# A top-4-of-32 expert layer: gathering tokens in 1 KB pieces and turning them with VectorE instead of TensorE

## Chip, cores and metric

One Trainium2 chip, one of its cores. The metric is the device time of one execution in microseconds; the median of several runs counts.

## What is computed

One layer of a hybrid encoder on 512 tokens plus 16 meta tokens, 1024 channels. A first half (one input projection, a depthwise convolution branch, an mLSTM branch, an output projection) is not touched by the change. The second half is a mixture of experts:

```python
u2 = rms_norm(h, norm_ffn_g)                          # 512 rows of 1024 count
logits = u2 @ router_w + router_b
top_val, top_idx = lax.top_k(logits, 4); gates = softmax(top_val)
# for every expert e, on the tokens that chose it:
hcat = xb @ w1[e] + b1[e]                             # 1024 -> 2048
h_glu, h_lin = split(hcat); h_glu = min(h_glu, 7); h_lin = clip(h_lin, -7, 7)
act = h_glu * sigmoid(1.702 * h_glu) * (h_lin + 1)
y = act @ w2[e] + b2[e]                               # 1024 -> 1024
out = rms_norm(h + sum over the 4 of gate * y)
```

512 tokens choose 4 of 32 experts each, so an expert gets 64 tokens on average. All weights are float32: an expert's w1 and w2 are 12 MB.

## The kernel before, in words

The program is written engine by engine, with semaphores by hand; each engine runs its own list in order. Up to about 520 us it does the first half. Then it makes `u2` (L1995, VectorE), writes it to DRAM as `u2_rows` (L522), computes logits, picks four experts for every token and gives each token a place in its expert's list (`choose`, `find_slots`).

An expert is computed on 96 slots (`SLOTS`), in three groups of 32 (`TG`). The expert loop runs once over the 32 experts. For expert n:

- TensorE, L1619: `hidden(k, t)`, 8 k-steps by 3 slot groups by 4 column groups of w1 (four products side by side in the array, 32 output partitions each), stationary `xT`, moving w1 from the ring. The first five k-steps go k by k, the last three slot group by slot group. After the fifth k-step stand the bias products (L1639, L1645), which wait for all of the last expert's `y_out` (`y_made`).
- VectorE and ScalarE turn each slot group of hidden units into `actT` (L2118 to L2131; the last step is a 32x32 block transpose, L2131).
- TensorE, L1668: `second(t)`, 32 products a slot group, moving w2. Between `second(0)` and `second(1)` stands `x_transposes(n + 1)` (L1606): eight TensorE transposes of the gathered rows `xs` [96 partitions, 1024] of the next expert. ScalarE copies them to `xT` (L1123).
- VectorE adds the bias and writes `y_out` (L2144), after POOL's step counter `idx_step` says that the last expert's scatters have landed.
- GpSimd (POOL): for each expert it copies the index columns (L754, L706), waits until `xs` has been used, gathers the rows of expert n+2 with one indirect DMA of 96 rows of 4 KB (L700), then issues three indirect DMAs that scatter `y_out` as 1 KB pieces to DRAM (L766), waits for their landing (`y_stored`, then `carrier`, L695), and goes on.
- SyncE (SP) loads the weights through a ring of 12 chunks of 1 MB, 8 of w1 (L484) and 4 of w2 (L488), each as soon as `ring_used` says that the last expert's chunk has been used.

Expert 0 has no gather: its `xT` comes from products of `u2` with a one-hot matrix of slots, `in_slot` (L1551), copied by ScalarE (L1088). Expert 1's rows are gathered with `token_now` made by VectorE (L2071). From expert 2 on, the indices come from a table in DRAM. GpSimd fills it with 16 indirect DMAs (L717), reads it back with 1 + 12 DMAs (L734, L738), and makes `token_of` and `row_of` with four arithmetic instructions (L741 to L746); only then it enters its expert loop (L754 on), whose first gather is that of expert 2.

## Time and profile before

| | us |
|---|---|
| median of 3 runs | 1619.48 (1618.56 to 1621.51) |
| profiled execution, first to last instruction (span) | 1597.8 |
| median less span (start and end around it) | 21.7 |
| TensorE busy | 1571.5 (98% of the span) |
| VectorE, GpSimd, ScalarE busy | 649.7, 444.7, 384.0 |
| data moved by DMA | 493.10 MB |

The profile shows one execution; its whole device time is not listed apart from its span, so what lies around the span is taken as the difference to the median. TensorE is busy from start to end, at full clock almost throughout. The expert loop takes from 542 to about 1575 us. A busy TensorE does not say that it works at its best, and the DMA engines are close to fully busy in the loop as well, at some 400 to 420 GB/s.

### The profile page before, as it was taken

The page shows a single profiled execution, that of the slowest core. Times are in us where ns is not written, and L with a number is a line of the kernel's source. Part 1 is how long each engine was busy: PE and PEld are TensorE (multiplying, and loading weights), DVE is VectorE, ACT ScalarE, POOL GpSimd, SP SyncE. Part 2 cuts the span into 40 slices and gives each one's busy share as a digit, 9 for nine tenths or more (in the row PEclk, how much of TensorE's full clock was granted, in tenths as well). Part 3 has the DMA queues.
Part 4 walks back from the last instruction along what each step waited for, and adds up shares of the span by engine and source line. Part 5 has one row for each costly group of instructions (what it writes and reads, how often), then busy time and mean ns, then how long its engine had stood idle before and what let it go on. Part 6 is the DMA issues. An engine that isn't in the chain of part 4 may idle for free.

```text
span 1597.8 us, 38945 instructions
## 1 busy us (share of the span) xinstructions
PE 1571.5 (98%) x16458; PEld 902.0 (56%) x16458; DVE 649.7 (41%) x1249; ACT 384.0 (24%) x601; POOL 444.7 (28%) x513
## 2 busy tenths in 40 slices
PE   7999999999999999999999999999999999999997
PEld 6998988877889644334433344334433443344334
DVE  4799898016242742224222332233222322232248
ACT  5333134346222311111111121122112111211112
POOL 7334333462433642111211111111211121112114
PEclk9999999999999999999999999999999999999999
DMA  7553242321275699999999999999999999999995
GB/s 217 159 179 112 79 144 95 90 72 51 79 294 224 204 340 406 407 416 414 412 398 410 412 409 398 414 407 408 394 411 407 410 392 404 411 412 400 403 413 236
DMA packets 129781, 493.10 MB, mean 309 GB/s; under 512 B 14379, under 2 KB 72099, under 8 KB 79973
## 3 DMA queue, kind: packets, MB, share of 16 engines
q1 hardware_dynamic: 110932, 464.61, 74.6%
q0 software_dynamic: 9168, 16.78, 3.2%
q10 hardware_dynamic: 9632, 11.03, 2.2%
q8 instruction: 35, 0.57, 0.1%
q14 instruction: 14, 0.11, 0.0%
HBM read 476.32 MB, written 24.87 MB: 314 GB/s over the span
## 4 chain that ended last, share of the span: by engine, by line
PE 95%; POOL 1%; ACT 1%; SPq 1%; DMA 1%; DVE 1%; issue 0%; POOLq 0%; DVEq 0%; ACTq 0%
PE banks L1619 41%; PE banks L1147 27%; PE banks L1668 21%; PE banks L1606 2%; DMA stage<-in_w_in_dram 1%; PE banks L1551 0%; PE banks L1639 0%; SPq L461 0%; PE banks L1506 0%; POOL h_res L787 0%; PE banks L1379 0%; POOL w_lo L624 0%; POOL w_lo L633 0%; POOL small L611 0%; SPq L447 0%
## 5 line engine op out<-in xcount | busy, mean ns | idle before, releaser
L1619 PE MATMUL banks<-w_ring,xT 128*32 128x512 f32 x6144 | 670.9, 592 | 0.1
L1619 PEld LDWEIGHTS banks<-w_ring,xT 128*32 128x32 f32 x6144 | 197.8, 110 | 431.3 <-issue 422.4
L1668 PE MATMUL banks<-w_ring,actT 128*32 128x256 f32 x6144 | 343.9, 380 | 0.0
L1668 PEld LDWEIGHTS banks<-w_ring,actT 128*32 128x32 f32 x6144 | 195.3, 110 | 144.8 <-issue 19.3
L2118 DVE TENSOR_TENSOR hid<-banks,bias 128x512 f32<-128x512 f32 x96 | 63.8, 665 | 475.6 <-PE banks L1619 475.6
L633 POOL TENSOR_TENSOR w_lo<-stage,w_hi 128x2048 fp32r<-128x2048 f32 x38 | 175.3, 4614 | 258.0 <-ACT w_hi L832 258.0
L1147 PE MATMUL banks<-u_hi,w_hi 128*128 128x264 f32 (+1 forms) x528 | 176.8, 335 | 1.5 <-POOL w_lo L624 1.5
L1147 PE MATMUL banks<-u_hi,w_lo 128*128 128x264 f32 (+1 forms) x528 | 175.1, 332 | 0.0
L1147 PE MATMUL banks<-u_lo,w_hi 128*128 128x264 f32 (+1 forms) x528 | 174.7, 331 | 0.0
L706 POOL COPY token_now<-token_of 96x1 int32 x32 | 6.6, 205 | 541.0 <-PE banks L1606 540.9
L1108 ACT ACTIVATE bias<-banks 128x512 f32<-128x512 f32 x32 | 19.1, 598 | 568.4 <-PE banks L1639 568.4
L1809 DVE SCALAR_TENSOR_TENSOR banks<-conv_in,taps,banks 128x512 f32<-128x512 f32 x224 | 151.0, 747 | 0.1
L2144 DVE TENSOR_TENSOR y_out<-banks,bias 128x256 f32<-128x256 f32 x96 | 40.8, 425 | 229.5 <-PE banks L1668 228.3
L1147 PEld LDWEIGHTS banks<-u_hi,w_hi 128*128 128x128 f32 x528 | 99.6, 189 | 11.7 <-POOL w_lo L624 1.7
L1147 PEld LDWEIGHTS banks<-u_lo,w_hi 128*128 128x128 f32 x528 | 99.6, 189 | 10.1
L1147 PEld LDWEIGHTS banks<-u_hi,w_lo 128*128 128x128 f32 x528 | 99.6, 189 | 9.5 <-issue 0.2
L832 ACT ACTIVATE w_hi<-stage 128x2048 fp32r<-128x2048 f32 x40 | 76.4, 1910 | 105.6 <-PE banks L1147 99.0
L695 POOL TENSOR_TENSOR carrier<-carrier 1x1 f32<-1x1 f32 x161 | 33.3, 207 | 240.4 <-DMA y_rows<-y_out,row_now 152.5
L766 POOL DMA_INDIRECT y_rows<-y_out,row_now x93 | 93.5, 1005 | 15.2 <-issue 15.2
L1116 ACT ACTIVATE sig<-hid 128x256 f32<-128x256 f32 x96 | 40.0, 417 | 194.2 <-DVE hid L2119 194.2
L2128 DVE TENSOR_TENSOR act_v<-hid,sig 128x256 f32<-128x256 f32 x96 | 59.8, 623 | 3.5 <-DVE hid L2126 0.3
L1123 ACT ACTIVATE xT<-banks 128x384 f32<-128x384 f32 x64 | 27.9, 488 | 80.0 <-PE banks L1606 80.0
(311 smaller groups left out, 1586.7 us busy)
## 6 DMA issues: line engine op xcount, KB each, us to landing
w_ring<-in_expert_w_dram SPq DMA_DIRECT2D x384, 1024.0 KB, 17.6
stage<-in_w_in_dram SPq DMA_DIRECT2D x20, 1024.0 KB, 5.3
stage<-in_w_in_dram SPq DMA_DIRECT2D x16, 512.0 KB, 5.6
y_rows<-empty_row ACTq DMA_DIRECT2D x8, 1024.0 KB, 4.8
y_in<-y_rows SPq DMA_DIRECT2D x4, 2048.0 KB, 20.8
stage<-in_conv_pw_w_dram SPq DMA_DIRECT2D x4, 1024.0 KB, 5.2
stage<-in_mlstm_out_w_dram SPq DMA_DIRECT2D x4, 1024.0 KB, 5.2
stage<-in_w_out_dram SPq DMA_DIRECT2D x4, 1024.0 KB, 5.5
```

The source lines that it names most:

```text
L633: nc.gpsimd.tensor_tensor(w_lo[:, s], stage[:, s], w_hi[:, s].bitcast(F32), ALU.subtract).then_inc(w_lo_made[s], 1)
L695: nc.gpsimd.tensor_tensor(carrier[:, 1 + i:2 + i], carrier[:, 0:1], carrier[:, 0:1], ALU.add).then_inc(idx_step, 1)
L766: pool.indirect_dma_start(out=y_dram, out_offset=bass.IndirectOffsetOnAxis(ap=row_now[:, t:t + 1], axis=0), in_=y_out[:, t], in_offset=Non ...
L832: nc.scalar.activation(w_hi[:, s], stage[:, s], ACT.Copy).then_inc(w_hi_made[s], 1)
L1116: nc.scalar.activation(sig[:, t], hid[:, t, 0:GRP], ACT.Sigmoid, scale=ALPHA).then_inc(sig_made, 1)
L1147: last = nc.tensor.matmul(dst, l, r, start=(k == 0 and n == 0), stop=(k == KT - 1 and n == 2))
L1619: last = nc.tensor.matmul(banks[32 * g:32 * (g + 1), t].rearrange("p (c j) -> p c j", j=64), xT[:, k, 32 * t:32 * (t + 1)], units, start=k ...
L1668: last = nc.tensor.matmul(banks[32 * g:32 * (g + 1), 3 + t, 0:GRP], actT[:, t, k], w2_ring[k // 2][:, k % 2, GRP * g:GRP * (g + 1)], start ...
L1809: nc.vector.scalar_tensor_tensor(out=to, in0=src, scalar=taps[:, ct, w:w + 1], in1=acc, op0=ALU.mult, op1=ALU.add).then_inc(conv_step, 1)
L2118: own(nc.vector.tensor_tensor(hid[:, t], banks[:, t], bias1.rearrange("p h n -> p (h n)"), ALU.add))
L2128: own(nc.vector.tensor_tensor(act_v[:, t].rearrange("p (c q j) -> p c j q", q=2, j=32), lin.rearrange("p (c j q) -> p c j q", q=2, j=32), ...
L2144: nc.vector.tensor_tensor(y_out[:, t], banks[:, 3 + t, 0:GRP], bias2, ALU.add).then_inc(y_made, 1)
```

## The change

`x_transposes` on TensorE and the copies on ScalarE go. The gathered rows come as four pieces of 1 KB, one for each group of 32 partitions, with one indirect DMA for each slot group: three instructions of 128 pieces, to `xs` [128, 3, 256]. VectorE then turns them with three 32x32 block transposes straight into `xT`. For this `u2` is written with its columns grouped (four instructions of 256 columns for one of 1024), and the router's weights are loaded in the same order, with eight DMAs. A slot's position within its 32 partitions changes: slots 0 to 7 of a group lie four partitions apart (`SPREAD`, `TURNS`), then the next eight one further.

The table is read back with 16 DMAs of 8 partitions, waited for together, and followed by 15 arithmetic instructions on GpSimd. The load of `last_g` moves from SP to GpSimd. Expert 0's rows come from 48 products of 32 x 256 outputs and three VectorE transposes.

```diff
+SPREAD = 8
+TURNS = 32 // SPREAD
...
-        token_of = in_stage("token_of", [SLOTS, PASSES * NE + 2], I32)
-        row_of = in_stage("row_of", [P, TG, PASSES * NE + 1], I32)
-        token_now = in_stage("token_now", [SLOTS, 1], I32)
-        token_part = in_stage("token_part", [SLOTS, PASSES * NE + 2])
+        piece_of = in_stage("piece_of", [P, TG, PASSES * NE + 2], I32)
+        row_of = in_stage("row_of", [P, TG, PASSES * NE + 2], I32)
+        piece_now = in_stage("piece_now", [P, TG], I32)
         row_now = in_stage("row_now", [P, TG], I32)
-        xs = in_stage("xs", [SLOTS, D])
-        xT = in_stage("xT", [P, KT, SLOTS])
+        xs = in_stage("xs", [P, TG, GRP])
+        xT = in_stage("xT", [P, TG, KT, 32])
...
-            sp.dma_start(w_router, router_w[0].rearrange("(k p) e -> p k e", p=P)).then_inc(router_in, 16)
+            for h in range(2):
+                for k in range(CG):
+                    sp.dma_start(w_router[32 * k:32 * (k + 1), h::2],
+                                 router_w[0].rearrange("(h k g j) e -> h k j g e", h=2, k=CG, g=CG)[h, k]).then_inc(router_in, 16)
...
-                sp.wait_ge(u2_made, i + 1)
+                sp.wait_ge(u2_made, CG * (i + 1))
...
-            sp.wait_ge(dest_made, TT)
-            sp.dma_start(last_g, final_norm_g.rearrange("(a d) -> a d", a=1).to_broadcast([P, D])).then_inc(row_bc_in, 16)
...
-            nc.gpsimd.iota(slot_no, [[1, SLOTS]], base=0, channel_multiplier=0, allow_small_or_imprecise_dtypes=True)
+            nc.gpsimd.iota(slot_no, [[32, TG], [1, SPREAD], [SPREAD, TURNS]], base=0, channel_multiplier=0, allow_small_or_imprecise_dtypes=True)
...
-                pool.indirect_dma_start(out=xs, out_offset=None, in_=u2_dram,
-                                        in_offset=bass.IndirectOffsetOnAxis(ap=token_now, axis=0),
-                                        bounds_check=last_token, oob_is_err=False).then_inc(xs_in, 16)
+                for t in range(TG):
+                    pool.indirect_dma_start(out=xs[:, t], out_offset=None, in_=u2_pieces,
+                                            in_offset=bass.IndirectOffsetOnAxis(ap=piece_now[:, t:t + 1], axis=0),
+                                            bounds_check=last_piece, oob_is_err=False).then_inc(xs_in, 16)
 
             def gather(n, copied):
 
-                nc.gpsimd.tensor_copy(token_now, token_of[:, bass.ds(n, 1)]).then_inc(idx_step, 1)
+                nc.gpsimd.tensor_copy(piece_now, piece_of[:, :, bass.ds(n, 1)].rearrange("p t o -> p (t o)")).then_inc(idx_step, 1)
                 pool.wait_ge(idx_step, copied)
                 request_rows()
...
-            by_slot = table.rearrange("(q i e) o -> i q (e o)", i=SLOTS, e=NE)
-            pool.dma_start(token_of[:, 0:PASSES * NE].rearrange("i (q e) -> i q e", e=NE),
-                           by_slot).then_inc(table_in, 16)
+            by_turn = table.rearrange("(x b a e) o -> b a x (e o)", b=TURNS, a=SPREAD, e=NE)
             for g in range(CG):
-                for t in range(TG):
-                    pool.dma_start(row_of[32 * g:32 * (g + 1), t, 0:PASSES * NE].rearrange("i (q e) -> i q e", e=NE),
-                                   by_slot[32 * t:32 * (t + 1)]).then_inc(rows_in, 16)
-            pool.wait_ge(table_in, 16)
-            chain(nc.gpsimd.tensor_scalar(token_part, token_of, -1.5, 0.25, ALU.add, ALU.mult))
-            chain(nc.gpsimd.tensor_scalar(token_part, token_part, TO_WHOLE, None, ALU.add))
-            chain(nc.gpsimd.tensor_scalar(token_of, token_part, -TO_WHOLE, None, ALU.add))
+                for b in range(TURNS):
+                    pool.dma_start(code_of[32 * g + b:32 * (g + 1):TURNS], by_turn[b]).then_inc(rows_in, 16)
+            pool.wait_ge(rows_in, 16 * CG * TURNS)
+            for t in range(TG):
+                codes = code_of[:, t::TG]
+                pieces = piece_of[:, t, 0:PASSES * NE].rearrange("p (q e) -> p q e", e=NE)
+                rows = row_of[:, t, 0:PASSES * NE].rearrange("p (q e) -> p q e", e=NE)
+                chain(nc.gpsimd.tensor_scalar(token_part, codes, -1.5, 0.25, ALU.add, ALU.mult))
+                chain(nc.gpsimd.tensor_scalar(token_part, token_part, TO_WHOLE, None, ALU.add))
+                chain(nc.gpsimd.tensor_scalar(token_part, token_part, -TO_WHOLE, None, ALU.add))
+                nc.gpsimd.tensor_scalar(pieces, token_part, float(CG), group_of, ALU.mult, ALU.add)
+                chain(nc.gpsimd.tensor_scalar(rows, codes, float(CG), group_of, ALU.mult, ALU.add))
+            pool.dma_start(last_g, final_norm_g.rearrange("(a d) -> a d", a=1).to_broadcast([P, D])).then_inc(last_g_in, 16)
...
-            pool.wait_ge(rows_in, 16 * CG * TG)
-            chain(nc.gpsimd.tensor_scalar(row_of, row_of, float(CG), group_of, ALU.mult, ALU.add))
...
-                    pool.wait_ge(xs_used, n + 2)
+                    pool.wait_ge(xT_made, (n + 2) * TG)
...
-                    act.wait_ge(xs_used, n + 2)
-                    for m in range(2):
-                        nc.scalar.activation(xT[:, 4 * m:4 * m + 4], banks[:, m, 0:4 * SLOTS].rearrange("p (k s) -> p k s", s=SLOTS),
-                                             ACT.Copy).then_inc(xT_made, 1)
...
-            def first_rows(i, m):
+                n = m + 1
+                for g in range(CG):
+                    nc.tensor.matmul(banks[32 * g:32 * (g + 1), X_BANKS[m], 0:n * GRP].rearrange("p (t c) -> p t c", c=P), zeros[:, 0:32],
+                                     zeros.unsqueeze(1).to_broadcast([P, 2 * n, P]), start=True, stop=False, tile_position=(0, 32 * g))
+
+            def first_rows(i):
 
                 pe.wait_ge(in_slot_made, i + 1)
-                for k in range(4):
-                    col = P * (4 * m + k)
-                    last = nc.tensor.matmul(banks[:, X_BANKS[m], SLOTS * k:SLOTS * (k + 1)], u2[:, i, col:col + P], in_slot[:, i],
-                                            start=False, stop=i == TT - 1 and k == 3)
-                if i == TT - 1:
-                    last.then_inc(rows_mm if m == 0 else xs_used, 1)
+                for t in range(TG):
+                    for g in range(CG):
+                        last = nc.tensor.matmul(first_xs(t)[32 * g:32 * (g + 1)], in_slot[:, i, 32 * t:32 * (t + 1)],
+                                                u2[:, i, GRP * g:GRP * (g + 1)], start=False, stop=i == TT - 1 and t != 1, tile_position=(0, 32 * g))
+                    if i == TT - 1:
+                        last.then_inc(rows_mm, 1)
...
-            def x_transposes(n):
-
-                pe.wait_ge(xs_in, n * 16)
-                for k in range(KT):
-                    last = nc.tensor.transpose(banks[:, k // 4, SLOTS * (k % 4):SLOTS * (k % 4 + 1)], xs[:, P * k:P * (k + 1)],
-                                               ident[0:SLOTS, 0:SLOTS])
-                last.then_inc(xs_used, 1)
...
-                                                    xT[:, k, 32 * t:32 * (t + 1)], units,
+                                                    xT[:, t, k], units,
...
-                    second(0)
-
-                    pe.wait_ge(actT_made, n * TG + 2)
-                    x_transposes(n + 1)
-                    second(1)
-                    second(2)
+                    for t in range(TG):
+                        second(t)
...
-                nc.vector.scalar_tensor_tensor(out=u2[:, i], in0=h_res[:, i], scalar=h_rstd[:, i:i + 1], in1=gf_bc,
-                                               op0=ALU.mult, op1=ALU.mult).then_inc(u2_made, 1)
+                for g in range(CG):
+                    nc.vector.scalar_tensor_tensor(out=u2[:, i, GRP * g:GRP * (g + 1)].rearrange("p (k j) -> p k j", j=32),
+                                                   in0=of_group(h_res[:, i], g), scalar=h_rstd[:, i:i + 1], in1=of_group(gf_bc, g),
+                                                   op0=ALU.mult, op1=ALU.mult).then_inc(u2_made, 1)
...
+                dve.wait_ge(rows_mm, TG if t else 1)
+                nc.vector.transpose(xT[:, t].rearrange("p k s -> p (k s)"), first_xs(t)).then_inc(xT_made, 1)
...
-            nc.vector.tensor_scalar(token_now, banks[0:SLOTS, SECOND_BANK, 0:1], 0.0, None, ALU.add).then_inc(tables_made, 1)
+            for g in range(CG):
+                for t in range(TG):
+                    nc.vector.tensor_scalar(piece_now[32 * g:32 * (g + 1), t:t + 1], banks[32 * t:32 * (t + 1), SECOND_BANK, 0:1],
+                                            float(CG), float(g), ALU.mult, ALU.add).then_inc(tables_made, 1)
...
+                    dve.wait_ge(xs_in, (n + 1) * (16 * TG))
+                    for t in range(TG):
+                        nc.vector.transpose(xT[:, t].rearrange("p k s -> p (k s)"), xs[:, t]).then_inc(xT_made, 1)
```

How the change moves instructions, first on TensorE, in the loop over experts (from the last products of `hidden` to the end of `second`). Before:

```order
L1668 MATMUL banks<-w_ring_118,actT 32x256 x8
L1677 REGISTER_ALU
L1606 MATMUL banks<-ident,xs 128x96 x8
L1668 MATMUL banks<-w_ring_115,actT 32x256 x8
L1668 MATMUL banks<-w_ring_116,actT 32x256 x8
```

and now:

```order
L1668 MATMUL banks<-w_ring_118,actT 32x256 x8
L1663 REGISTER_ALU
L1668 MATMUL banks<-w_ring_115,actT 32x256 x8
L1668 MATMUL banks<-w_ring_116,actT 32x256 x8
```

The eight transposes between `second(0)` and `second(1)` are gone. On GpSimd, between the filling of the table and the loop over experts, before:

```order
L717 DMA slot_table<-code,dest 18432x1 x8
L695 TENSOR_TENSOR carrier<-carrier 1x1
L700 DMA xs<-u_rows,token_now 96x1024
L717 DMA slot_table<-code,dest 18432x1 x8
L734 DMA token_of<-slot_table 96x6x32
L738 DMA row_of<-slot_table 32x6x32 x12
L741 TENSOR_SCALAR token_part<-token_of 96x194
L742 TENSOR_SCALAR token_part<-token_part 96x194
L743 TENSOR_SCALAR token_of<-token_part 96x194
L746 TENSOR_SCALAR row_of<-row_of,group_of 128x579
```

and now, where the five rows L750 to L754 stand three times:

```order
L725 DMA slot_table<-code,dest 18432x1 x8
L701 TENSOR_TENSOR carrier<-carrier 1x1
L707 DMA xs<-u_rows,piece_now 128x256 x3
L725 DMA slot_table<-code,dest 18432x1 x8
L744 DMA code_of<-slot_table 8x18x32 x16
L750 TENSOR_SCALAR token_part<-code_of 128x192
L751 TENSOR_SCALAR token_part<-token_part 128x192
L752 TENSOR_SCALAR token_part<-token_part 128x192
L753 TENSOR_SCALAR piece_of<-token_part,group_of 128x192
L754 TENSOR_SCALAR row_of<-code_of,group_of 128x192
...
L755 DMA last_g<-in_final_norm_g_dram 128x1024
```

Three gathers stand for one, 16 table loads for 13, 15 arithmetic instructions for 4, and the load of `last_g` is new here. On VectorE, at the end of an expert, before:

```order
L2131 STREAM_TRANSPOSE actT<-act_v 128x256
L2141 ISA
L2144 TENSOR_TENSOR y_out<-banks,bias_170 128x256 x3
```

and now:

```order
L2134 STREAM_TRANSPOSE actT<-act_v 128x256
L2142 ISA
L2144 STREAM_TRANSPOSE xT<-xs 128x256 x3
L2147 ISA
L2150 TENSOR_TENSOR y_out<-banks,bias_171 128x256 x3
```

The three transposes of the next expert's rows, with their wait for the gathers (`xs_in`), now stand ahead of the three `y_out` additions.

## Rows read from the trace of the kernel before

**Rows 1.** The page: span and busy time of each engine.
```profile
span 1597.8 us, 38945 instructions
...
PE 1571.5 (98%) x16458; PEld 902.0 (56%) x16458; DVE 649.7 (41%) x1249; ACT 384.0 (24%) x601; POOL 444.7 (28%) x513
```

**Rows 2.** Timeline, TensorE: start us, us, engine, line, operation, tiles, count.
```profile
606.59 13.06 PE L1619 MATMUL banks<-w_ring,xT 128*32 128x512 f32 x120
631.10 0.88 PE L1606 MATMUL banks<-ident,xs 96*128 96x96 f32 x8
631.91 7.11 PE L1668 MATMUL banks<-w_ring,actT 128*32 128x256 f32 x128
638.84 6.62 PE L1619 MATMUL banks<-w_ring,xT 128*32 128x512 f32 x60
```

**Rows 3.** Stretches: PE, PEld, DVE, ACT, POOL busy; PEclk, DMA share, GB/s.
```profile
605.00:610.00 5.00, 5.00 (x68) 1.95 (x60) 0.43 (x1) 0.00 (x0) 1.41 (x3) 1.00 1.01 332
610.00:614.00 4.00, 4.00 (x44) 1.28 (x40) 0.00 (x0) 0.00 (x0) 0.19 (x2) 1.00 1.03 420
614.00:637.00 23.00, 23.00 (x304) 9.81 (x299) 8.66 (x20) 5.67 (x10) 3.46 (x8) 1.00 1.01 422
606.77:639.03 32.26, 32.26 (x405) 13.21 (x400) 9.08 (x21) 5.67 (x10) 5.32 (x11) 1.00 1.02 407
```

**Rows 4.** Loads of w1 into the ring (L484), 600 to 700 us.
```profile
DMA to landing us min/median/max: 15.2/17.4/19.4
```

**Rows 5.** The same, 1300 to 1500 us.
```profile
DMA to landing us min/median/max: 17.2/20.2/22.9
```

**Rows 6.** Timeline, 884 to 911 us: ring loads issued, products they are for.
```profile
884.22 2.05 SPq L484 DMA_DIRECT2D w_ring<-in_expert_w_dram  x3
910.09 7.91 PE L1619 MATMUL banks<-w_ring,xT 128*32 128x512 f32 x72
```

**Rows 7.** Timeline, VectorE, end of an expert (idle before, and what ended it).
```profile
888.45 0.45 DVE L2131 STREAM_TRANSPOSE actT<-act_v 128x256 f32<-128x256 f32 x1
889.34 0.42 DVE L2144 TENSOR_TENSOR y_out<-banks,bias 128x256 f32<-128x256 f32 x1 [0.44 <-PE banks L1668]
```

**Rows 8.** Timeline, GpSimd, before the expert loop.
```profile
550.04 1.03 POOL L700 DMA_INDIRECT xs<-u_rows,token_now  x1 [0.16 <-issue]
568.44 0.82 POOL L734 DMA_DIRECT2D token_of<-slot_table  x1 [7.20 <-DMA slot_table<-code,dest]
569.26 6.81 POOL L738 DMA_DIRECT2D row_of<-slot_table  x12
576.09 0.39 POOL L741 TENSOR_SCALAR token_part<-token_of 96x194 f32<-96x194 int32 x1
576.56 0.74 POOL L742 TENSOR_SCALAR token_part<-token_part 96x194 f32<-96x194 f32 x1
577.38 0.70 POOL L743 TENSOR_SCALAR token_of<-token_part 96x194 int32<-96x194 f32 x1
584.67 0.77 POOL L746 TENSOR_SCALAR row_of<-row_of,group_of 128x579 int32<-128x579 int32 x1 [6.59 <-DMA row_of<-slot_table]
586.75 0.19 POOL L754 COPY row_now<-row_of 128x3 int32 x1 [1.30 <-issue]
587.81 1.11 POOL L700 DMA_INDIRECT xs<-u_rows,token_now  x1 [0.40 <-issue]
```

**Rows 9.** The scatters of expert rows (L766): issue to landing.
```profile
DMA to landing us min/median/max: 5.6/7.3/8.7
```

**Rows 10.** Stretches as in rows 3: two with a lower clock.
```profile
345.00:355.00 10.00, 9.82 (x37) 7.22 (x36) 1.71 (x4) 4.55 (x8) 10.00 (x7) 0.83 0.02 6
1592.00:1598.00 6.00, 0.00 (x0) 0.00 (x0) 2.70 (x3) 0.00 (x0) 1.63 (x2) 0.50 0.65 255
```

**Rows 11.** Timeline, 539 to 543 us: VectorE before expert 0, TensorE at its start.
```profile
539.40 1.01 DVE L2026 SCALAR_TENSOR_TENSOR in_second<-slot_no,banks,mask 128x96 f32<-128x96 f32 x4
542.06 13.08 PE L1619 MATMUL banks<-w_ring,xT 128*32 128x512 f32 x120
```

More of the change, by code:

```diff
@@ L243, in hybrid_block @@
         last_g = at("last_g", [P, D], F32, ffn_at[0])
+        one_hot_at = ffn_at[0]
         one_hot = in_stage("one_hot", [P, TT, TOPK, NE])
@@ L1586, in _ @@
             places(1)
-            for m in range(2):
-                first_rows(0, m)
+            first_rows(0)
             places(2)
-            for m in range(2):
-                first_rows(1, m)
+            first_rows(1)
             places(3)
@@ L1594, in _ @@
             for i in range(2, TT):
-                for m in range(2):
-                    first_rows(i, m)
+                first_rows(i)
             pe.wait_ge(in_slot_made, 2 * TT)
```

39 lines of the change are left out of this document (21 added, 18 removed).

## Prediction

> **What bounds the kernel now.** I read the page first: TensorE is busy for 98% of the span [rows 1], so only what shortens TensorE's own list, or makes it wait, moves the end. The timeline of TensorE gives the rhythm of the expert loop: expert 2 starts at 606.59 and expert 3 at 638.84, a period of 32.25 us, with no idle time in it [rows 2]. The eight transposes of the next expert's rows start at 631.10 and the next product at 631.91: they hold 0.81 us of each period [rows 2].
>
> Then the stretches, for what TensorE leans on. Over one period the DMA engines are busy throughout (share 1.02) and move 407 GB/s, which is 13.13 MB. For most of the period they run at 422 GB/s, and for 5 us around the gather and the scatters at 332 [rows 3]. This dip costs 5 x (422 - 332) / 422 = 1.07 us a period. Without it 13.13 MB would take 31.1 us, with it 32.2. So the DMA engines are as full as TensorE. They even lose a little: the median from issue to landing of a w1 chunk grows from 17.4 us [rows 4] to 20.2 [rows 5], 2.8 us over some 22 experts, 0.13 us an expert. I take 32.35 us an expert for the DMA engines.
>
> How much slack is there? The third of the chunks issued from 884.22 goes out at about 885.9, and its product starts at 910.09 [rows 6]: 24.2 us. The slowest landing is 19.4 us early [rows 4] and 22.9 late [rows 5], which leaves 4.8 us early in the loop and 1.3 late. Two rates must therefore be forecast, TensorE's and the DMA engines'.
>
> **TensorE.** Without its transposes the period is 32.25 - 0.81 = 31.44 us. Over 31 experts that is -25.1 us. The 32nd is counted with the tail, below.
>
> **DMA engines.** The bytes stay the same: 64 rows of 4 KB become 256 pieces of 1 KB. The unknown is the dip. Bounds: all of it goes (31.1 to 31.2 us), or all of it stays (32.35). The gather writes 64 of 96 partitions, each 4 KB; now the same bytes are spread over 128 partitions, and the part-filled third group of slots over all of its 32. From 610 to 614, where only scatters of 1 KB pieces are left to land, the rate is back at 420 [rows 3], so it is the stretch with the gather that is slow. I take more than half of the dip as gone, 31.6 us. This is under the point that matters: over 29 experts TensorE can stay ahead of the DMA engines by the slack of 4.8 us plus the stall found below (6.7), 0.4 us an expert, so anything up to 31.84 costs nothing. The sum takes 0.
>
> The Trainium skill (SBUF — State Buffer, Door 1: The DMA port swizzle) says that partitions 0 to 63 reach only 8 of the 16 DMA ports. By it, 0.26 MB at half the ports would hold these for 0.6 us longer than when spread, so 0.6 us of the dip would go, and the DMA engines would need about 31.75 us; no run here shows it yet.
>
> **VectorE.** It gets three transposes an expert. One of the same shape takes 0.45 us [rows 7], three in a row about 1.2. They stand before `y_out`, which now starts at 889.34; it starts about 1 us later. TensorE asks for `y_out` only at the fifth k-step of the next expert, and VectorE idles most of the period (9.1 of 32.3 us busy [rows 3]): nothing. ScalarE's two copies go from beside the path: nothing.
>
> **GpSimd, once, before the loop.** This is where I expect a stall. Expert 2's rows are the first that need the table. In the kernel before GpSimd enters the loop at 586.75 and gathers at 587.81 [rows 8]. Now it is later by:
> - two more gathers for expert 1, each 1.03 us and a gap of 0.3: +2.6
> - 16 table loads of 0.57 each (12 took 6.81) for 0.82 + 6.81: +1.5
> - 15 arithmetic instructions for one after the landing. L742 and L743, with one operation each, start 0.82 apart; L741 and L746 with two operations are cheaper (0.47 to the next start, and 0.77 for 579 columns, so 0.35 for 192). A round is 0.47 + 0.82 + 0.82 + 0.35 + 0.4 = 2.9, three are 8.6, less the 0.77 that stood there: +7.8
> - the load of `last_g`, as L734: +0.8
>
> Together 12.7 us, all from rows 8; the wait for the loads' landing stays as it was (6.59 us). The first gather starts at 600.5, the third 2.6 later at 603.1. The nearest row for the landing is that of the scatters, 7.3 us (5.6 to 8.7) [rows 9]: 610.4. With 1.2 for the transposes `xT` is there at 611.6. TensorE reaches expert 2 at 606.59 - 2 x 0.81 = 605.0. It stalls for 6.6 to 6.7 us. Lower bound: all arithmetic at the price of the cheap form (15 x 0.4) and a landing of 5.6 give 2.4. Upper: all at 0.82, and 8.7, give 12. I take the middle, as each part has a row. Behind it VectorE and GpSimd are late too, but both have 20 us to catch up: `y_out` of expert 1 waits for scatters that land near 615, and the bias products of expert 2 come near 622. After that a gather is issued a whole expert ahead again, and the extra 2.6 us of GpSimd an expert lie in idle time.
>
> Such a stall may cost clock as well. At the end of the program, where TensorE has nothing left, the granted clock is 0.50 (1.2 for 2.4 GHz). The one earlier drop, among products on few rows, gives a mean of 0.83 over 10 us, so it took 1.7 us of full-speed work [rows 10]. Bounds 0 and 1.7; I take +1.0.
>
> **Expert 0 and the tail.** The 48 one-hot products and VectorE's transposes replace 32 wider ones and ScalarE's copies. VectorE is at `in_second` until 540.41; with three transposes after it, it is ready at about 541.6, and expert 0 starts at 542.06 [rows 11]: 0, between -0.3 and +1. Seven more router loads stand on SP ahead of the load of the norm's weights; an issue is at most 0.7 us (2.05 for three [rows 6]), and TensorE is still in the first half's products: 0, at worst +2. The four-part `u2` costs VectorE 0.2 us beside its waits: 0. In the last expert the three transposes delay the sums by 1.2 us, against TensorE's 0.81: +0.4.
>
> **Sum.** -25.1 + 6.7 + 1.0 + 0.4 = -17.0 on a span of 1597.8, so 1580.8. The median of the runs stands 21.7 above the span, which gives 1602.5 us, 1.05% less. For this case alone the range is 1597 to 1609.
>
> **Rivals.**
> - No stall: table and gathers are faster than their rows say. Then 1619.5 - 25.1 + 0.4 = 1595. Against it: four separate delays would all have to shrink. 0.10.
> - The dip shrinks by less than half. Between 31.84 and 32.35 us an expert the DMA engines set the pace after some ten experts, and the time lies between 1603 and 1618, at 32.1 about 1610. For it: the scatters lie in the same 5 us. 0.15.
> - The change does nothing for the path: the dip stays whole, the chunks come at 32.35 us an expert, TensorE is faster and waits for them. Only the late slack is won: 1619.5 - 1.3 = 1618. 0.07.
> - Slower: 256 pieces cost the DMA engines more than 64 rows, read at scattered addresses and asked for by four times the descriptors. It decides from 32.35 us an expert on. If the dip becomes half as dear again, 32.9 us: 31 x 0.65 - 1.3 = +18.9, 1638. Against it: the scatters already move 1 KB pieces, in the same full stream. 0.10. The Trainium skill (DMA: Bandwidth & Descriptors, Why small descriptors are slow) gives a fixed 3 cycles a descriptor; on 32 beats for 1 KB this would be 0.06 us an expert, and the rival would fall.
>
> My own case keeps 0.58.
>
> **How the numbers follow.** A measurement here can tell about 0.2%, 3.2 us, from no change. Faster takes my case, the case without a stall and the second rival, 0.83, less 0.01 for that one's upper end. That 0.01 and 0.10 make 0.11 slower, for a slow DMA case milder than the one priced, and the unchanged case is the 0.07 of same. The range reaches from the case without a stall, 1594, to 1617 at the end of the partly bound one; beyond it lie the slower case and the unchanged one, under 2 in 10.
>
> **What would show it.** In the loop: a period of 31.44 us, no L1606 rows, a DMA rate in the dip well above 332 GB/s, and chunk landings that do not grow. Before expert 2: one idle time of TensorE of 3 to 12 us ended by VectorE's `xT`, and GpSimd's first copy of `row_now` near 599.4. The forecast is wrong if TensorE waits for ring chunks in many experts (the DMA rivals), or if expert 2 starts without a gap.

## The result, and the profile after

The changed kernel took 1672.06 us, median of 4 runs (1670.03 to 1673.62), beside 1620.49 us (1618.56 to 1622.12) of the kernel before: a ratio of 1.032, 95% interval 1.0305 to 1.0336. It is slower by 3.2%. The forecast of 1602.5 us was wrong in sign, and the time lies outside the range.

The pair was measured again later, and there it came out the other way: 1579.74 us (1578.32 to 1581.08) beside 1598.48 us, ratio 0.9883, interval 0.9866 to 0.9899. Which chip the recorded pair ran on is not on record, so its difference to the later runs may lie in the chip or in the time; below, "the other chip" is the one of this second measurement. So two questions stand: whether the forecast's steps describe the kernel, and what the recorded pair met that the later runs did not. Both profiles follow, the recorded one first.

The page of the recorded run: span, busy time of TensorE, and the groups of the second products and their weight loads (busy, mean ns | idle before, what ended it).

```profile
span 1671.8 us, 38588 instructions
...
PE 1619.7 (97%) x16240; PEld 1139.5 (68%) x16240; DVE 682.7 (41%) x1371; ACT 355.0 (21%) x535; POOL 520.9 (31%) x594
...
L1668 PE MATMUL banks<-w_ring,actT 128*32 128x256 f32 x6144 | 415.9, 380 | 17.3 <-issue 3.0
L1668 PEld LDWEIGHTS banks<-w_ring,actT 128*32 128x32 f32 x6144 | 293.7, 110 | 141.9 <-issue 112.6
```

The same lines of the same kernel on the other chip, in a profiled run of 1581.08 us.

```profile
span 1579.3 us, 38588 instructions
...
PE 1541.0 (98%) x16240; PEld 900.7 (57%) x16240; DVE 682.7 (43%) x1371; ACT 355.2 (22%) x535; POOL 522.2 (33%) x594
...
L1668 PE MATMUL banks<-w_ring,actT 128*32 128x256 f32 x6144 | 337.6, 379 | 0.0
L1668 PEld LDWEIGHTS banks<-w_ring,actT 128*32 128x32 f32 x6144 | 209.8, 110 | 135.3 <-issue 18.7
```

The instructions are as many, and one second product lasts 380 ns in the one and 379 in the other. Their busy total, in which products that overlap count once, is 78 us longer in the recorded run, and the weight loads stand idle 112.6 us for "issue", which is time in which nothing the profile shows held them. On the other chip that is 18.7 us.

Where in an expert is it? The timeline of the recorded run: TensorE, and its weight loads at the end of the second products.

```profile
981.90 13.63 PE L1668 MATMUL banks<-w_ring,actT 128*32 128x256 f32 x192
995.22 3.31 PE L1619 MATMUL banks<-w_ring,xT 128*32 128x512 f32 x28
...
988.48 1.84 PEld L1668 LDWEIGHTS banks<-w_ring,actT 128*32 128x32 f32 x31
990.79 0.20 PEld L1668 LDWEIGHTS banks<-w_ring,actT 128*32 128x32 f32 x6 [0.48 <-issue]
991.53 0.17 PEld L1668 LDWEIGHTS banks<-w_ring,actT 128*32 128x32 f32 x4 [0.55 <-issue]
992.25 0.16 PEld L1668 LDWEIGHTS banks<-w_ring,actT 128*32 128x32 f32 x5 [0.55 <-issue]
```

Up to 990.8 us the products follow each other at full pace, then they come four to six at a time, every 0.72 us, until just before the next expert begins. I call these the bursts. The 192 products take 13.63 us. GpSimd's timeline at that time:

```profile
987.29 1.06 POOL L707 DMA_INDIRECT xs<-u_rows,piece_now  x1 [0.36 <-issue]
988.66 1.03 POOL L707 DMA_INDIRECT xs<-u_rows,piece_now  x1 [0.30 <-issue]
989.99 1.00 POOL L707 DMA_INDIRECT xs<-u_rows,piece_now  x1 [0.30 <-issue]
991.01 0.18 POOL L701 TENSOR_TENSOR carrier<-carrier 1x1 f32<-1x1 f32 x1
991.35 1.03 POOL L776 DMA_INDIRECT y_rows<-y_out,row_now  x1 [0.16 <-issue]
```

The bursts lie beside GpSimd's row of indirect DMAs, 3.5 us behind its start. A whole period, and the 5 us with the bursts of the expert before, as stretches (columns as in [rows 3]):

```profile
960.93:995.22 34.29, 33.75 (x399) 22.54 (x393) 9.96 (x24) 4.80 (x8) 7.43 (x13) 1.00 0.94 383
...
955.00:960.00 5.00, 4.56 (x48) 1.74 (x39) 0.42 (x1) 0.00 (x0) 3.81 (x6) 1.00 0.59 231
```

The period is 34.29 us, 2.85 over the forecast of 31.44. The clock is full. The DMA engines are busy for 59% of the stretch with the bursts: the ring is loaded, and its next loads wait for TensorE. So neither the clock nor the DMA engines hold it.

The start of the expert loop in the same trace says more. TensorE in expert 0 and at the start of expert 2; GpSimd at the end of a row of eleven indirect DMAs (552.10 to 569.05 us) and behind it; the stretch from 566 us:

```profile
565.02 2.49 PE L1619 MATMUL banks<-w_ring,xT 128*32 128x512 f32 x9 [0.34 <-issue]
567.88 1.06 PE L1619 MATMUL banks<-w_ring,xT 128*32 128x512 f32 x3 [0.37 <-issue]
569.31 2.95 PE L1619 MATMUL banks<-w_ring,xT 128*32 128x512 f32 x12 [0.36 <-issue]
572.11 10.29 PE L1668 MATMUL banks<-w_ring,actT 128*32 128x256 f32 x182
...
616.78 14.09 PE L1619 MATMUL banks<-w_ring,xT 128*32 128x512 f32 x118
...
568.05 1.00 POOL L725 DMA_INDIRECT slot_table<-code,dest  x1 [0.31 <-issue]
570.51 9.69 POOL L744 DMA_DIRECT2D code_of<-slot_table  x16 [1.47 <-DMA slot_table<-code,dest]
...
566.00:572.00 6.00, 4.89 (x26) 1.16 (x27) 3.69 (x9) 0.42 (x1) 3.92 (x6) 1.00 0.04 5
```

The last eight DMAs of the row write single numbers to the table. Beside them the products of `hidden` are held up too, 24 in 7.2 us, at a DMA share of 0.04. The second products of expert 0 that follow have no burst, without any pause in them, while GpSimd issues plain loads. So in this trace the bursts go with GpSimd's indirect DMAs, not with a place in TensorE's list and not with many bytes. And expert 2 starts at 616.78 without a gap: the forecast stall is not in the recorded run, where TensorE itself is late by then.

Now the other chip: TensorE at the end of expert 1 and the start of expert 2, the stretches of a later period and of its gather, and the landings of w1 chunks, early (600 to 700 us) and late (1300 to 1500 us).

```profile
593.22 10.54 PE L1668 MATMUL banks<-w_ring,actT 128*32 128x256 f32 x192
611.27 15.12 PE L1619 MATMUL banks<-w_ring,xT 128*32 128x512 f32 x120 [7.51 <-DVE xT L2144]
...
895.11:926.42 31.31, 31.31 (x397) 13.59 (x393) 10.02 (x24) 4.80 (x8) 7.42 (x14) 1.00 1.02 418
...
925.00:930.00 5.00, 5.00 (x68) 2.15 (x64) 0.42 (x1) 0.00 (x0) 3.70 (x7) 1.00 1.01 395
...
DMA to landing us min/median/max: 4.8/9.3/17.1
...
DMA to landing us min/median/max: 6.9/11.8/12.5
```

The period is 31.31 us without idle time, where [rows 2] have 32.25. The dip at the gather and the scatters is 395 GB/s, where [rows 3] have 332. The chunks land 6.9 to 12.5 us after their issue late in the loop, where [rows 5] have 17.2 to 22.9. And there is the one idle time of TensorE that was forecast, 7.51 us before expert 2.

### The profile page after: what moved, and what is told of

It is laid out like the page before. It is cut to its first block, busy times and chain, and to the rows that moved or that the text cites. A ratio compares the mean times of both kernels' runs of the same rounds, so it can differ in the third digit from the quotient of the medians.

```text
span 1671.8 us, 38588 instructions
## 1 busy us (share of the span) xinstructions
PE 1619.7 (97%) x16240; PEld 1139.5 (68%) x16240; DVE 682.7 (41%) x1371; ACT 355.0 (21%) x535; POOL 520.9 (31%) x594
## 4 chain that ended last, share of the span: by engine, by line
PE 92%; DVE 2%; issue 2%; POOL 1%; ACT 1%; SPq 1%; DMA 1%; another core or an unknown queue 0%; POOLq 0%; DVEq 0%; ACTq 0%
PE banks L1619 39%; PE banks L1156 26%; PE banks L1668 24%; DMA stage<-in_w_in_dram 1%; DVE bias_rest L2080 0%; PE banks L1639 0%; SPq L467 0%; PE banks L1515 0%; POOL h_res L797 0%; PE banks L1388 0%; POOL w_lo L630 0%; POOL w_lo L639 0%; POOL small L617 0%; SPq L453 0%
## 5 line engine op out<-in xcount | busy, mean ns | idle before, releaser
L1619 PE MATMUL banks<-w_ring,xT 128*32 128x512 f32 x6144 | 686.7, 592 | 3.5 <-DVE bias_rest L2080 1.4
L1619 PEld LDWEIGHTS banks<-w_ring,xT 128*32 128x32 f32 x6144 | 359.0, 110 | 282.4 <-issue 241.5
L1668 PE MATMUL banks<-w_ring,actT 128*32 128x256 f32 x6144 | 415.9, 380 | 17.3 <-issue 3.0
L1668 PEld LDWEIGHTS banks<-w_ring,actT 128*32 128x32 f32 x6144 | 293.7, 110 | 141.9 <-issue 112.6
L713 POOL COPY piece_now<-piece_of 128x3 int32 x32 | 6.0, 187 | 522.4 <-DVE xT L2144 522.4
L707 POOL DMA_INDIRECT xs<-u_rows,piece_now x99 | 106.2, 1073 | 32.0 <-issue 32.0
```

The source lines that it names most:

```text
L707: pool.indirect_dma_start(out=xs[:, t], out_offset=None, in_=u2_pieces, in_offset=bass.IndirectOffsetOnAxis(ap=piece_now[:, t:t + 1], axis=0),
L1619: last = nc.tensor.matmul(banks[32 * g:32 * (g + 1), t].rearrange("p (c j) -> p c j", j=64), xT[:, t, k], units, start=k == 0, stop=k == K ...
L1668: last = nc.tensor.matmul(banks[32 * g:32 * (g + 1), 3 + t, 0:GRP], actT[:, t, k], w2_ring[k // 2][:, k % 2, GRP * g:GRP * (g + 1)], start ...
```

## The experiments

Theories on the bursts: **A**, a row of indirect DMAs on GpSimd slows the rate at which TensorE gets its instructions. **B**, without the transposes nothing pauses TensorE in the second products, and its supply runs out whatever GpSimd does. **C**, the bytes of the gathered pieces slow it. **D**, the recorded pair met a condition, of its chip or of its time, that the later runs are not in. Each set of runs went to a chip of its own, seven in all, with the kernel before beside it. A changed kernel given without a ratio was run once; runs of one kernel on one chip lie up to 3.6 us apart.

**The gathers behind the scatters.** On GpSimd, per expert:

```
-   gather(n + 2)            ahead of the three scatters
+   gather(n + 2)            behind the three scatters
```

> In the changed kernel an expert takes 34.3 us, 2.9 us over the 31.44 us of the forecast, and the trace shows where: the last 37 or so of the 192 second products are issued in bursts of four every 0.72 us. Those bursts start about 3 us after the first of the three gathers. Theory A: a row of indirect DMAs on GpSimd (three gathers, then three scatters) slows the rate at which TensorE gets its instructions, and the second products, the shortest ones, need the highest rate. Theory B: with the transposes gone nothing pauses TensorE in the second products, and its supply runs out after some 155 pairs whatever GpSimd does. Theory C: the gathered pieces' bytes, written beside the products, slow them. Here the three gathers are issued behind the three scatters, in the next expert's hidden products. A and C: the bursts leave the second products; hidden products are issued at half the rate and may hide most of it, so the period falls to between 31.4 and 33 us and the time to between 1583 and 1632 us. B: the bursts stay where they are, period 34.3 us, time 1668 to 1676 us.

Measured: 1585.44 us, against 1598.9 for the kernel before (0.9914, 0.9898 to 0.9931). The bursts are gone, but so they would have been anyway: 1598.9 where the recorded pair had 1620.5 said that this run was not in its condition. The run decided nothing until the changed kernel had run beside it.

**One gather instead of three.**

```
-   for t in range(TG):
+   for t in range(1):
        pool.indirect_dma_start(out=xs[:, t], ...)
```

> Of the three gathers of an expert only the first is issued; slots of the other two turns keep zeros, so their part of the result is missing, and the products and transposes are as many as before. A: one gather and three scatters, as the kernel before the change has them, leave TensorE's supply alone: no bursts, period 31.4 to 32 us, time 1582 to 1600 us. B: unchanged, 1668 to 1676 us. C: a third of the bytes is left, so a third of the 2.9 us: period near 32.4 us, time near 1612 us.

Measured: 1572.31 us. TensorE's wait before expert 2 was 3.0 us instead of 7.5. No bursts, where the kernel before shows that the condition is absent.

**Two more gathers in the kernel before.**

```
+   for m in range(2):
+       pool.indirect_dma_start(out=extra[m], in_=table, in_offset=token_now, ...)
```

> The kernel before the change, with two more indirect gathers of 96 rows behind each expert's own one; each row is one 4-byte number, so that there are hardly any bytes. A: bursts appear in the second products of this kernel too, 1 to 3 us an expert, time 1650 to 1710 us. B: the transposes' pause is still there, so nothing changes, 1617 to 1625 us. C: hardly any bytes, nothing changes, 1617 to 1625 us.

Measured: 1602.31 us, 3.4 us over the kernel before, and no bursts. A misses its 1650 to 1710; for B and C, which expected no change, it is nearly none.

**The changed kernel and the one before, again.**

> The changed kernel as it is, beside the kernel before. In the last set of runs the kernel before took 1598.9 us where it had taken 1620.5, which is 1.1 us over its profiled span of 1597.8 us; so the 21.7 us that the forecast put around the span may have been a chip that ran the loop otherwise. If the bursts belong to the kernel alone (theory B, and A as it stood), the changed kernel shows them here too: a period of 34.3 us and 1660 to 1674 us. If they need a chip in that condition as well (theory D: one chip supplies TensorE's instructions more slowly than another), the bursts are shorter or absent and the time lies between 1575 and 1640 us.

> The kernel before the change, for a second profile. If its time is near 1600 us, its span will be 1 to 2 us less and its period 32.2 us; if near 1620 us, either the span is again 1598 us and 22 us lie outside, or the span is 1618 us and the period 32.9 us, which places the 21 us in the loop.

Measured: 1579.74 us (0.9883, 0.9866 to 0.9899), and 1598.45 us with a span of 1596.7. The changed kernel has no bursts here, which is the low end of D. Span and run are 1.8 us apart for both kernels.

> The gathers behind the scatters once more, to stand beside the changed kernel on the same chip. A: 1580 to 1590 us on a chip where the kernel before takes 1599, and 30 to 90 us less than the changed kernel wherever that one shows bursts. D without bursts: within 5 us of the changed kernel.

Measured: 1584.57 us (0.9913, 0.9897 to 0.993), 4.8 us more than the changed kernel on the same chip. The wait before expert 2 is 11.5 us instead of 7.5, since expert 2's gather now stands behind expert 0's scatters.

> The changed kernel with its three gathers set apart: the first at its old place, the second behind the first scatter, the third behind the second scatter. As many indirect DMAs, the last four still close to one another at the end of the expert. A, if it is the gathers' place beside the second products: the bursts begin later, period 32 to 33.5 us, time 1600 to 1640 us. B: as the changed kernel. D without bursts: within 5 us of the changed kernel.

```
    for t in range(TG):
        (scatter of turn t)
+       if t < TG - 1: request_rows([t + 1])
```

Measured: 1583.04 us (0.9905, 0.9889 to 0.9922), wait before expert 2 10.2 us. Within 5 us, as D has it. Neither order helps where no bursts are.

**Fewer loads of the table.** From here on the runs test the forecast's own terms. The edit is one constant:

```
-SPREAD = 8
+SPREAD = 32
```

> The changed kernel with its slots in plain order (turns of 32 slots instead of 8), so that GpSimd loads its table with 4 transfers instead of 16. The fresh profile of the changed kernel (span 1579.3 us) shows the one idle stretch that was forecast: TensorE waits 7.51 us before expert 2 for the gather that GpSimd issued late, at 600.60 us, and the 120 products behind it take 15.12 us instead of 13.06, with the clock at half for 6.8 us of them. If the lateness of GpSimd is the cause: 12 loads fewer at 0.61 us are 7.3 us, so the wait falls to 0.2 us, the clock stays up, and the time is 9.4 us less than the changed kernel's 1579.7 us, 1570 us (1568 to 1573), against the kernel before 0.982. If the even dealing of slots is worth something in each expert, some of it is lost again: 0.1 us an expert would give 1573 us. On a chip where the kernel before takes 1620 us: bursts as in the first profile, 1655 to 1672 us.

> Turns of 16 slots, 8 loads of the table: 8 loads fewer at 0.61 us are 4.9 us, which leaves a wait of 2.6 us before expert 2. If the half clock comes with any such wait, its 2.1 us stay: 1574.8 us; if a short wait leaves the clock up: 1572.8 us. If the dealing of slots costs or brings nothing in the loop, this lies between the changed kernel and the one with plain order.

Measured: 1572.25 us with plain order (0.9834, 0.9818 to 0.985) and 1575.19 us with turns of 16 (0.9849, 0.9833 to 0.9866). TensorE's timeline before expert 2, plain order first, then turns of 16:

```profile
605.55 13.08 PE L1619 MATMUL banks<-w_ring,xT 128*32 128x512 f32 x120 [0.95 <-DVE xT L2144]
```

```profile
606.60 14.78 PE L1619 MATMUL banks<-w_ring,xT 128*32 128x512 f32 x120 [2.36 <-DVE xT L2144]
```

The wait fell from 7.51 to 2.36 and 0.95 us. After 2.36 us of it 120 products still took 14.78 us instead of 13.08; after 0.95 us the clock stayed up. The stretches behind the wait, turns of 16 first, then plain order:

```profile
608.00:610.00 2.00, 2.00 (x16) 0.56 (x12) 0.48 (x2) 0.00 (x0) 0.18 (x1) 0.50 1.01 420
```

```profile
605.50:615.00 9.50, 9.45 (x88) 2.98 (x92) 1.08 (x3) 0.00 (x0) 5.35 (x11) 1.00 1.02 419
```

So GpSimd's lateness is the cause of the stall. Each is within 2.5 us of its forecast. The even dealing of slots is worth nothing that shows: the period is the same. Plain order is faster by 2.9 us here, but the times of the two overlap (1571.02 to 1573.81 and 1572.8 to 1576.25 us), and a second profile of plain order, below, has the longer wait as well.

**The transposes back.**

```
    second(0)
+   for k in range(KT):
+       nc.tensor.transpose(banks[...], ident[0:SLOTS], ident[0:SLOTS, 0:SLOTS])
    second(1)
```

> The changed kernel with eight transposes of a constant put back between the second products of turn 0 and turn 1, where the kernel before had its own; their results are not used. The forecast priced them at 0.81 us an expert, 32 times: about 1579.7 + 26 = 1605.6 us (1602 to 1608). If the period is then set by the DMA engines (theory R, in which transposes were hidden beside the transfers), hardly anything is added, 1580 to 1590 us. On a chip where the kernel before takes 1620 us, theory B expects the pause to take the bursts away, 1600 to 1625 us, and theory A expects them to stay, 1680 to 1700 us.

Measured: 1610.81 us, 2.8 us over the expected range. The chain of waits of this kernel, one expert's part (start us, us, what):

```profile
958.79 3.45 PE banks L1668 x64
962.25 0.81 PE banks L1679 x8
963.06 7.04 PE banks L1668 x128
970.10 12.88 PE banks L1619 x120
```

With the transposes the second part takes 3.45 + 0.81 + 7.04 = 11.30 us, without them 10.36 (the chain's rows of the kernel with plain order). The transposes cost 0.94 us an expert: 0.81 of their own, and 0.13 for the products being cut in two. Over 32 experts this is 30.1 us, where 26 were expected. Theory R falls: they are not hidden beside the transfers. The kernel is 11.9 us slower than the one before beside it: the 1 KB pieces bring nothing while TensorE keeps transposes, and the stall before expert 2 (6.6 us here) is left.

**Twelve indirect DMAs in a row, and none.**

```
    (three gathers of an expert)
+   for m in range(6):
+       pool.indirect_dma_start(out=extra[m], in_=table, in_offset=piece_now[:, 0:1], ...)
```

> The changed kernel with six more indirect gathers of 4-byte rows behind each expert's three, so that GpSimd issues twelve indirect DMAs in a row, over 16 us of each expert. On a chip where the kernel before takes 1599 us the changed kernel shows no bursts. Theory A in its general form (the closer together GpSimd's indirect DMAs, the slower TensorE's supply, on every chip) expects bursts here: 2 to 8 us an expert, 1640 to 1830 us. Theory D (the chip of the recorded pair was in a condition that these are not in, and the indirect DMAs only met it) expects none: 1579 to 1584 us, the packets' own time on the DMA engines being small. On a chip where the kernel before takes 1620 us: A and D both expect 1700 us or more, B 1672 us.

> The changed kernel without any indirect DMA in the loop: gathers and scatters of the experts are left out, so the experts work on old rows and their results are not stored; every product, transpose and weight load stays. With no dip at the gather and the scatters, and 20 MB less to move, this shows what the indirect DMAs cost TensorE. If TensorE sets the period alone, the period stays at 31.32 us, and with the stall before expert 2 gone (9.6 us) the time is about 1570 us (1568 to 1572). If the transfers still cost something, it is less, down to 1555 us. On a chip where the kernel before takes 1620 us: A expects no bursts, 1565 to 1575 us; B expects 1660 to 1672 us.

Measured: 1586.34 us and 1567.88 us, beside 1597.39 for the kernel before. With twelve indirect DMAs in a row there is no burst, and TensorE's second products take 10.36 us as with none (chain of waits, first of the kernel with twelve, then of the one without any):

```profile
948.18 10.36 PE banks L1675 x192
```

```profile
937.02 10.36 PE banks L1663 x192
```

A in its general form falls. The first kernel's 1586.34 us are 6.6 over the changed kernel's on another chip, and over the expected 1579 to 1584; its list of waits has TensorE wait 8.3 us before expert 2 and 2.4 us, in four places, for ring chunks. The second kernel shows that in the changed kernel the gathers and scatters cost TensorE nothing in the loop: without any indirect DMA the period is 31.3 us as well.

**The transposes out of the kernel before.**

```
    def x_transposes(n):
        pe.wait_ge(xs_in, n * 16)
-       for k in range(KT):
-           last = nc.tensor.transpose(banks[...], xs[:, P * k:P * (k + 1)], ...)
-       last.then_inc(xs_used, 1)
+       pe.sem_inc(xs_used, 1)
```

> The kernel before the change with its eight TensorE transposes of gathered rows left out, so the products of experts 1 to 31 use other numbers; the 4 KB gather, ScalarE's copies and all waits stay. This is the removed work alone, without the 1 KB pieces. The runs so far give 0.93 us an expert for the transposes (32.25 against 31.32 us). If TensorE alone sets the period here too: 1598 - 32 x 0.93 = 1568 us (1566 to 1571). If the dip of one large gather on the DMA engines holds the period above 31.32, as the forecast's DMA sum for the old gather has it (32.2 us with the dip, 31.1 without), hardly anything is gained: 1585 to 1598 us. Where the kernel before takes 1620 us: B expects bursts and a gain of less than nothing, 1640 us or more; A expects 1590 us, 29 us less.

Measured: 1593.63 us beside 1598.89. Of the 30 us that the transposes cost, 5.3 come back. The waits of TensorE; stretches with the gather and without it; the landings of the ring's chunks from 900 to 965 us:

```profile
PE banks L1616 <- DMA w_ring<-in_expert_w_dram: 17.9, 24, 1.1
...
945.00:950.00 5.00, 5.00 (x100) 3.66 (x96) 2.29 (x6) 2.57 (x4) 2.67 (x5) 1.00 1.01 421
950.00:955.00 5.00, 5.00 (x92) 3.32 (x86) 0.85 (x2) 0.00 (x0) 1.35 (x3) 1.00 1.01 355
...
DMA to landing us min/median/max: 18.6/22.4/26.0
```

TensorE waits for ring chunks 24 times, 17.9 us in all: from expert 6 on the DMA engines set the period, about 32.2 us (two steps of the chain of waits, from 911.63 to 976.12 us, are 64.5). That is the second of the two outcomes. The 4 KB gather's dip is back, 355 GB/s. Two changes are needed together, as this run and the one with the transposes back show: the transposes go from TensorE's list, and with the 1 KB pieces most of the dip goes from the DMA engines.

> The changed kernel with its gathers but without the experts' scatters, so the experts' results are not stored. Where the kernel before takes 1598 us: period 31.32 us as with and without all indirect DMAs, the stall before expert 2 as in the changed kernel, 1577 to 1582 us. Where it takes 1620 us: A expects shorter bursts, about half, 1610 to 1640 us; B expects 1672 us.

```
-   pool.indirect_dma_start(out=y_dram, ..., in_=y_out[:, t], ...)
```

Measured: 1581.73 us, wait before expert 2 7.1 us, second products 10.36 us: as expected, and silent on the bursts.

**Looking for the condition.** Three more kernels went to a fifth chip, and after the two of the last paragraphs one to a seventh.

> The changed kernel once more, on what may be another chip. Where the kernel before takes 1597 to 1600 us: 1578 to 1581 us, no bursts. Where it takes 1620 us: 1668 to 1674 us with bursts, which would place the difference in the chip and not in the day.

> No indirect DMAs in the loop, as in the run before. Where the kernel before takes 1600 us: 1567 to 1569 us. Where it takes 1620 us: if the bursts need GpSimd's indirect DMAs, 1565 to 1575 us; if they come without them, 1655 us or more.

> Slots in plain order, the shortest of the complete kernels so far. Where the kernel before takes 1600 us: 1571 to 1574 us. Where it takes 1620 us: 1655 to 1668 us with bursts.

> The changed kernel on one more chip, as the last attempt to meet the condition of the recorded pair. Where the kernel before takes 1597 to 1600 us: 1578 to 1583 us. Where it takes 1620 us: 1668 to 1674 us if that condition belongs to a chip.

Measured: 1582.54, 1568.70 and 1575.89 us beside 1597.54, then 1580.39 us beside 1597.94 (0.9889, 0.986 to 0.9918). The condition did not come up again. Two of the four miss their ranges: the changed kernel by 1.5 us, with a wait of 8.2 us before expert 2, and plain order by 1.9 us. Its row before expert 2:

```profile
606.44 14.78 PE L1619 MATMUL banks<-w_ring,xT 128*32 128x512 f32 x120 [2.46 <-DVE xT L2144]
```

So the same kernel waits 0.95 us in one profile and 2.46 in another, and with the longer wait the slower 120 products are back.

## Why the prediction was wrong

**The step that failed in the recorded run is TensorE's period.** The forecast had "Without its transposes the period is 32.25 - 0.81 = 31.44 us" and put nothing for the rate at which TensorE issues its products. Measured in its place: 34.29 us. That is 2.85 us more in each of 31 experts, 88 us, against the 91.0 us by which the profiled span (1671.8) exceeds the forecast one (1580.8). The forecast's next two terms, +6.7 for the stall and +1.0 for the clock, did not come up there at all: "if expert 2 starts without a gap" was one of its own signs of being wrong.

**The base failed too.** The step was "The median of the runs stands 21.7 above the span, which gives 1602.5 us". I took 21.7 us as time around the span. In every run with both on record the two are 1.7 to 1.8 us apart (1581.08 and 1579.3, 1598.45 and 1596.7), in the recorded changed kernel as well (1673.57 and 1671.8). So the profile of before was in all likelihood of an execution near 1600 us, and the timed runs beside it were 20 us slower somewhere that this profile does not show. That gap was visible ahead of the forecast and should have widened the range on both sides.

**What the bursts cost, and what is open.** From the start of expert 2 to that of expert 31 the recorded run takes 1614.06 - 616.78 = 997.3 us and the other chip's 1521.80 - 611.27 = 910.5: 86.8 us, 3.0 an expert, of the 92.3 us between 1672.06 and 1579.74. The other 5.5 us come before expert 2, where bursts cost more than the missing stall saves. It is shown that the kernel alone does not bring the bursts (the same kernel on three other chips), that the missing pause alone does not either (B falls the same way, and expert 0's second products have none in the recorded trace), and that twelve indirect DMAs in a row don't make them without the condition. In the recorded profile they lie beside the indirect DMAs ahead of the loop too: 48 one-hot products (L1562) took 4.21 us from 537.05 while GpSimd wrote its table, and 2.80 us on the other chip. That they need the indirect DMAs is read from where they lie in one trace; no run in the condition took the DMAs away. What the condition is stays open, and so does whether the pause or the single gather protected the kernel before, which was 22 us slower in it: no kernel but the recorded pair ran in it. How TensorE's instructions reach it, and whether that way was slow, no run looked at.

**On the other chips the sum can be held against its terms.** It was -17.0 us; the runs give 1579.74 - 1598.48 = -18.7, the profiled spans 1579.3 - 1596.7 = -17.4. So close a match is partly luck, as the terms show.
- TensorE, -25.1: right in kind, too small. The transposes cost 0.94 us, not 0.81, as cutting the second products costs 0.13 more, and all 32 count: -30.1.
- DMA engines, 0 as long as they need under 31.84 us: right. 418 GB/s over 31.31 us are 13.1 MB a period. The dip shrank from 332 to 395 GB/s and costs 5 x (423 - 395) / 423 = 0.33 us instead of 1.07. That is 0.74 us won, by windows of 5 us; over whole periods the rate is 418 against 407 GB/s. The rule of the Trainium skill (SBUF — State Buffer, Door 1: The DMA port swizzle) gave an estimate of 0.6 us; by that rule, the trace agrees in size. Whether the ports or the size of the pieces did it was not tried apart. With the 4 KB gather the period is 32.2 us when the DMA engines set it, where 32.35 was forecast.
- GpSimd's lateness: right. Its first gather for expert 2 starts at 600.60 us (forecast 600.5), the third at 603.36 (603.1), and TensorE waits 7.51 us (6.7); 7.4 and 8.2 us on two more chips.
- Clock, +1.0 between 0 and 1.7: too small. The 120 products behind the stall take 15.12 us instead of 13.06, 2.1 us (14.44 and 15.74 us on two more chips).
- Expert 0, 0: right. It starts at 540.94 us in the changed kernel and 540.98 in the kernel before, both from the second profiles.
- The tail, +0.4: +3.1 is what the spans leave for it. 0.4 us of this lie ahead of the last store, as forecast: it goes out 20.1 us earlier, where the three terms above give 20.5. The other 2.7 us stand behind the last store, as the last section shows.

-30.1 + 7.5 + 2.1 + 3.1 = -17.4. The gain on TensorE was put 5 us too low, and the losses (stall, clock, tail) 4.6 us too low together, and the errors cancelled. The steps are of the right kind; that their sum comes out within 0.4 us is luck. Of the rivals, none was the recorded result. The case without a stall and the one in which less than half of the dip goes are refuted by 7.51 us and by 0.33 of 1.07 us left; the slower one, dearer 1 KB pieces, by the DMA engines' having got faster.

## What to carry to other kernels

Hold a profile's span against the timed runs before building on it: a gap of 22 us where 2 are usual is a sign that the profile shows another kind of execution than the one to be predicted, and a verdict from one set of runs may not hold in the next. When TensorE and the DMA engines are equally full, taking work from one gives nothing alone (5 of 30 us here); look for an edit that relieves both, and then for the serial start that it makes longer. Here another constant, which cuts the table's loads from 16 to 4, gave another 6.7 us on the one chip that ran both kernels (1582.54 and 1575.89 us, one run each); at 0.983 of the kernel before it is the fastest complete kernel of this study.

## What the runs showed of the hardware

In one condition TensorE issued its instructions in groups of mostly four to six pairs every 0.72 us at full clock, with no wait for an operand on record and the DMA engines partly idle; the profile calls it "issue". Against the other chips the changed kernel lost 92 us in it and the kernel before 22, and none of the later sets of runs, on seven chips, showed it.

Behind waits of 2.36 and 2.46 us TensorE ran at half clock (a granted clock of 0.50 from 608 to 610 us in the kernel with turns of 16) for part of the next 120 products, behind one of 0.95 us it did not. The stretch behind the stall of 7.51 us in the changed kernel on the other chip has a mean clock of 0.54:

```profile
609.00:616.00 7.00, 4.73 (x28) 1.23 (x32) 2.18 (x6) 0.00 (x0) 1.75 (x5) 0.54 1.01 420
```

The stores of the result, first of the kernel before, then of the changed one, both from the second profiles:

```profile
L570 SPq DMA_DIRECT2D out_dram<-h_res x5: 332/333/346, 1586.7 to 1594.2; - x5
```

```profile
L576 SPq DMA_DIRECT2D out_dram<-h_res x5: 332/333/346, 1566.7 to 1574.1; - x5
```

The last store goes out 20.1 us earlier, and in both kernels it lands within 2.6 us; but the span ends at 1596.7 in the one and at 1579.3 in the other, 2.5 and 5.2 us behind that issue. With one gather an expert or none it ends 2.5 or 2.6 us behind the issue too; with three gathers of 1 KB pieces it is 5.1 to 5.3 us, in the recorded run as well, 6.8 without the scatters, 3.5 with six small gathers added, and 4.0 in the kernel before with two small ones added. No row shows what runs in that time. The 2.7 us between the two are what the tail term missed.
